# Turning the router's rows in 32x32 blocks on VectorE instead of transposing them on TensorE, in a pool, convolution and mixture-of-experts layer

## The reference, cut to what matters

```python
h = layer_norm(x, ln_in_g, ln_in_b)
mix = hybrid_mixer(h, w_in, pool_w, pool_scale, conv_w, conv_b, w_out)
    # h @ w_in; pooled windows on one half, gated short convolution on the other; @ w_out
h = layer_norm(ALPHA * h + mix, ln1_g, ln1_b)              # called h1 below
probs = softmax(h @ w_router)                              # 16 experts
# the best group of four experts, in it the two best; gates from their probabilities
ffn = grouped_moe(h, ...)          # silu(x @ w1[e]) * (x @ w3[e]) @ w2[e], blocks of 128 rows
h = layer_norm(ALPHA * h + ffn, ln2_g, ln2_b)
```

## Time and the profile before

| what | value |
|---|---|
| median of 3 runs | 1347.22 us (1345.38 to 1347.94) |
| the profiled execution | 1347.38 us, its span in the trace 1345.5 us |
| TensorE busy | 1310.9 us, 97% |
| VectorE busy | 969.2 us, 72% |
| ScalarE busy | 510.8 us, 38% |
| GpSimd busy | 515.4 us, 38% |
| DMA | 243.59 MB, mean 181 GB/s |

### The profile page before, as it was taken

How to read it: one execution, slowest core, us unless ns; L and a number is a source line. 1 busy time by engine, 2 the same in 40 slices (tenths; PEclk the granted TensorE clock), 3 DMA queues, 4 the chain that set the end, 5 groups by cost and what they waited for, 6 DMA issues and landing times.

```text
span 1345.5 us, 20470 instructions
## 1 busy us (share of the span) xinstructions
PE 1310.9 (97%) x6382; PEld 1096.3 (81%) x6383; DVE 969.2 (72%) x1358; ACT 510.8 (38%) x568; POOL 515.4 (38%) x543
## 2 busy tenths in 40 slices
PE   5999999999999999998999999999999999999995
PEld 5888888888888888887888888888888888888884
DVE  7758577687759786698777885775775677777574
ACT  3423234322343234324444554433442454443351
POOL 2001110111101010022566665656555556665655
PEclk9999999999999999999999999999999999999998
DMA  9625434564455344544877774564555545766421
GB/s 271 177 87 164 147 108 169 163 192 117 156 178 167 111 141 146 208 184 167 307 263 266 264 264 145 190 231 140 183 196 186 184 169 210 237 235 233 152 70 64
DMA packets 156523, 243.59 MB, mean 181 GB/s; under 512 B 18944, under 2 KB 84992, under 8 KB 156480
## 3 DMA queue, kind: packets, MB, share of 16 engines
q1 hardware_dynamic: 118624, 154.15, 35.0%
q0 software_dynamic: 28928, 71.74, 15.1%
q10 hardware_dynamic: 8928, 17.13, 3.7%
HBM read 211.97 MB, written 64.62 MB: 206 GB/s over the span
## 4 chain that ended last, share of the span: by engine, by line
PE 94%; DVE 2%; issue 1%; DMA 1%; POOL 1%; DVEq 0%; ACT 0%; SPq 0%; POOLq 0%
PE acc L520 28%; PE acc L522 28%; PE acc L521 28%; PE tp L560 4%; PE logits L599 2%; PE aux L830 1%; DMA b_in<-in_ln_in_b 1%; PE logits L645 0%; DVE ring_lo L1650 0%; DMA xg<-h_scratch,gat_now 0%; DVE ring_lo L1239 0%; PE aux L522 0%; PE aux L521 0%; PE aux L520 0%; PE aux L670 0%
## 5 line engine op out<-in xcount | busy, mean ns | idle before, releaser
L520 PE MATMUL acc<-ring_hi 128*128 128x512 f32 (+1 forms) x800 | 309.1, 386 | 1.8 <-DVE ring_lo L1239 1.6
L522 PE MATMUL acc<-ring_hi,ring_lo 128*128 128x512 f32 (+1 forms) x800 | 305.7, 382 | 0.0
L521 PE MATMUL acc<-ring_lo,ring_hi 128*128 128x512 f32 (+1 forms) x800 | 305.4, 382 | 0.0
L520 PE MATMUL acc<-ring_hi,xt_hi 128*128 128x512 f32 x648 | 256.4, 396 | 2.4 <-issue 2.2
L522 PE MATMUL acc<-ring_hi,xt_lo 128*128 128x512 f32 x648 | 252.8, 390 | 0.0
L521 PE MATMUL acc<-ring_lo,xt_hi 128*128 128x512 f32 x648 | 252.5, 390 | 0.0
L1803 POOL TENSOR_TENSOR small<-small 128x1 f32<-128x1 f32 x31 | 47.4, 1528 | 360.8 <-DVE small L1208 360.8
L520 PEld LDWEIGHTS acc<-ring_hi 128*128 128x128 f32 x800 | 151.4, 189 | 29.9 <-DVE ring_lo L1239 2.4
L522 PEld LDWEIGHTS acc<-ring_hi,ring_lo 128*128 128x128 f32 x800 | 151.3, 189 | 29.1
L521 PEld LDWEIGHTS acc<-ring_lo,ring_hi 128*128 128x128 f32 x800 | 151.5, 189 | 27.6
L1650 DVE TENSOR_TENSOR ring_lo<-stage_x,ring_hi 128x2048 fp32r<-128x2048 f32 x60 | 161.2, 2727 | 0.2
(11 more groups left out here) (277 smaller groups left out, 1922.7 us busy)
## 6 DMA issues: line engine op xcount, KB each, us to landing
stage_x<-in_exp_w SPq DMA_DIRECT2D x64, 1024.0 KB, 6.9
stage<-in_w_in SPq DMA_DIRECT2D x64, 512.0 KB, 5.4
stage<-in_exp_w SPq DMA_DIRECT2D x32, 1024.0 KB, 7.1
stage<-in_w_out SPq DMA_DIRECT2D x32, 512.0 KB, 5.1
h_scratch<-hres POOLq DMA_DIRECT2D x16, 512.0 KB, 3.0
sum_scratch<-hres ACTq DMA_DIRECT2D x16, 512.0 KB, 2.9
hrow<-in_x POOLq DMA_DIRECT2D x12, 512.0 KB, 4.7
h_scratch<-hrow POOLq DMA_DIRECT2D x12, 512.0 KB, 3.0
```

Source lines behind the costliest of these rows:

```text
L520: nc.tensor.matmul(dst, w_hi, x_hi, start=start, stop=False)
L521: nc.tensor.matmul(dst, w_hi, x_lo, start=False, stop=False)
L522: return nc.tensor.matmul(dst, w_lo, x_hi, start=False, stop=stop)
```

## The change

The h1 tiles of the first three routed chunks are no longer transposed by TensorE. ScalarE scales and stores a tile at step `t + 1` already, then loads the unscaled tile back from `h1_dram` into the same place in `hres` at step `t + 2`, in four quarters (`h1_back`): partition quarter `a` gets columns 256a to 256a + 255 of all 128 rows, in pieces of 1 KB. VectorE turns the tile at step `t + 3` with one instruction, in 32x32 blocks, into `h1t` (`h1_turn`, last in the step before the next chunk's layer norm). Column `8 c + k` of the 1024 now lies in block `k`, so `wr` is loaded in that order, and the last chunk's transposes read `hres` with a step of 8. The router matmuls move between the two sections of steps 4 to 7. The residual load of a tile is issued at step `t + 4` and waits for its turn.

```diff
-                if t == 0 and c > 1:
-                    pe.wait_ge(s_h1tc, (c - 1) * TPC * 2)
...
-            def h1_tile(c, t):
-
-                pe.wait_ge(s_h1, c * TPC + t + 1)
-                if t >= 1:
-                    pe.wait_ge(s_h1tc, (c * TPC + t) * 2)
-                transpose_tile(hres[:, t, :], s_h1t)
-
             def route_tile(c, t):
-                pe.wait_ge(s_h1tc, (c * TPC + t + 1) * 2)
+                pe.wait_ge(s_h1turn, c * TPC + t + 1)
...
             def h1_last(t, k):
-                mm = nc.tensor.transpose(last_banks[t % 2][k // 4][:, k % 4, :], hres[:, t, k * P:(k + 1) * P], ident[:])
+                by_k = hres[:, t, :].rearrange("p (c k) -> p k c", k=KT)
+                mm = nc.tensor.transpose(last_banks[t % 2][k // 4][:, k % 4, :], by_k[:, k, :], ident[:])
...
                         section(slot, which, sct).then_inc(s_sec[sct], 1)
+                        if not first and which == 0 and j >= 4:
+                            route_tile(c - 1, j - 4)
...
-                    if not first:
-                        if 3 <= j < 7:
-                            route_tile(c - 1, j - 3)
-                        if 2 <= j < 6:
-                            h1_tile(c - 1, j - 2)
...
-            def h1t_copy(c, t):
-                if c >= 1 and t == 0:
-                    act.wait_ge(s_lst, c)
-                for b in range(2):
-
-                    act.wait_ge(s_h1t, (c * TPC + t) * 2 + b + 1)
-                    nc.scalar.copy(h1t[:, 4 * b:4 * b + 4, :], tp[b][:]).then_inc(s_h1tc, 1)
-
             def alpha_h1(c, t):
 
                 act.wait_ge(s_h1out[t], c * 16 + 16)
-                act.wait_ge(s_h1t, (c * TPC + t + 1) * 2)
+                if c == NCH - 1:
+                    act.wait_ge(s_h1t, (t + 1) * 2)
...
+            def h1_back(c, t):
+
+                act.wait_ge(s_ahout[t], c * 16 + 16)
+                rows = h1_dram[(c * TPC + t) * P:(c * TPC + t + 1) * P, 0:D].rearrange("(r b) (a f) -> a r b f", r=SUB, a=QUARTERS)
+                for a in range(QUARTERS):
+                    dst = hres[a * SUB:(a + 1) * SUB, t, :].rearrange("r (b f) -> r b f", b=QUARTERS)
+                    act.dma_start(dst, rows[a]).then_inc(s_h1q[t], 16)
+
             def res_load(c, t):
 
+                act.wait_ge(s_h1turn, (c - 1) * TPC + t + 1)
...
-                act.dma_start(wr[:], w_router.rearrange("(k p) e -> p k e", p=P)).then_inc(s_const, 16)
+                act.dma_start(wr[:], w_router.rearrange("(p k) e -> p k e", p=P)).then_inc(s_const, 16)
...
-                    if not first and 3 <= j < 7:
-                        h1t_copy(c - 1, j - 3)
+                    if not first and 1 <= j < 5:
+                        alpha_h1(c - 1, j - 1)
+                    if not first and 2 <= j < 6:
+                        h1_back(c - 1, j - 2)
                     if not first and 4 <= j < 8:
-                        alpha_h1(c - 1, j - 4)
-                    if not first and 5 <= j < 9:
-                        res_load(c, j - 5)
+                        res_load(c, j - 4)
...
+
+            def h1_turn(c, t):
+
+                dve.wait_ge(s_h1q[t], (c + 1) * 16 * QUARTERS)
+                dve.wait_ge(s_log, c * TPC + t)
+                if c >= 1 and t == 0:
+                    dve.wait_ge(s_lst, c)
+                V.transpose(h1t[:].rearrange("p k (r b) -> p k b r", r=SUB),
+                            hres[:, t, :].rearrange("p (b c k) -> p k b c", b=QUARTERS, c=SUB)).then_inc(s_h1turn, 1)
...
                     if j < 8 and j % 2 == 1:
                         gate_rows(c, g)
+                    if not first and 3 <= j < 7:
+                        h1_turn(c - 1, j - 3)
```

More of the change, by code:

```diff
@@ L64 @@
 ROW = D + NE
+SUB = 32
+QUARTERS = P // SUB
 ALIGN = 128
@@ L384, in build @@
         s_h1t = sem("h1_transposed")
+        s_h1q = [sem(f"h1_quarters_in{t}") for t in range(TPC)]
+        s_h1turn = sem("h1_quarters_turned")
         s_h1tc = sem("h1_t_copied")
@@ L633, in h1_ready @@
                 elif t >= 2:
-                    pe.wait_ge(s_h1tc, (LAST * TPC + t - 1) * 2)
+                    pe.wait_ge(s_h1tc, (t - 1) * 2)
             def h1_last(t, k):
-                mm = nc.tensor.transpose(last_banks[t % 2][k // 4][:, k % 4, :], hres[:, t, k * P:(k + 1) * P], ident[:])
+                by_k = hres[:, t, :].rearrange("p (c k) -> p k c", k=KT)
+                mm = nc.tensor.transpose(last_banks[t % 2][k // 4][:, k % 4, :], by_k[:, k, :], ident[:])
                 if k % 4 == 3:
@@ L642, in route_last @@
                 if k % 4 == 0:
-                    pe.wait_ge(s_h1tc, (LAST * TPC + t) * 2 + k // 4 + 1)
+                    pe.wait_ge(s_h1tc, t * 2 + k // 4 + 1)
                 tile = LAST * TPC + t
@@ L1077, in _ @@
                 for b in range(2):
-                    act.wait_ge(s_h1t, ((NCH - 1) * TPC + t) * 2 + b + 1)
+                    act.wait_ge(s_h1t, t * 2 + b + 1)
                     if t >= 2:
```

## The result

The changed kernel takes 1415.82 us (median of 4 runs, 1414.07 to 1416.72) beside 1346.54 us for the kernel before: ratio 1.0513, 95% interval 1.0499 to 1.0528, 69.3 us slower. Forecast were 1395 us and at most 1413. The direction and the mechanism came as predicted; the size lies outside the range. The profiled execution has a span of 1414.6 us, 69.1 more than before.

A forecast was written before the change was run, and what follows sets the result against it. TensorE, with 94% of the chain that ended last, was taken as the bound. Stalls 54.0, less 10.9 for removed transposes, plus 3.9 slow clock and 1.0 last chunk, gave +48.0 us: 1395 us, range 1383 to 1413.

The forecast's parts named there:

- the three long waits: TensorE's router tile 0 waits for VectorE's turn once in each of three chunks: 18.6, 17.7 and 17.7 us, together 54.0.
- the ring: ScalarE, VectorE, GpSimd and an h1 store wait on one another once a step; 50.3 us until tile 0 is turned.
- The last chunk's transposes: 32 TensorE transposes kept in the last chunk, reading hres with a step of 8: 1.0 us more, bounds 0 to 3.5.
- each chunk some 14 us longer: A sign named in advance: how much longer each chunk would take if the forecast held.
- first step: ScalarE's issue of a tile's four quarter loads, priced as a plain load's 0.43 us each: 1.7 us a tile.
- The two ScalarE links: ScalarE's scaling, quarter issues and copies before layer norm 2 and before the turn of tile 0: 4.4 and 5.3 us.
- The landings in the ring: Three h1 stores a chunk reach DRAM before ScalarE can go on: 3.0 us each, bounds 2.9 to 4.0.
- the turn: VectorE's new transpose of a 128x1024 f32 tile, counting the strided reading only: 1.9 us, bounds 1.3 to 2.7.
- second step: TensorE running at half clock behind each of three stalls: 1.3 us each, 3.9 us in all, bounds 0 and twice that.
- C: Rival: only VectorE's order counts, ScalarE's waits fit its slack; three stalls of 5.1 us, +7, 1355 us; chance 0.06.
- B: Rival: stores, quarters and scaled stores collide with unit loads; three landings a chunk 2 us longer, 1413 us; chance 0.09.
- D: Rival: tile 0 is turned when TensorE arrives, so the full 10.9 us come back, 1336.5 us; chance 0.03.

The follow-up runs named there:

- experiment 3: Changed kernel with ScalarE's scaling and store, quarter loads and residual load moved behind its bank copies of the same step: 1364.96 us, ratio 1.0146 to the kernel before.
- experiment 11: Kernel before the change, with only the stepped reading of h1 in all 128 TensorE transposes and router weights loaded to match: 1348.57 us, ratio 1.0012.
- experiment 1: Changed kernel with one plain load of a tile in place of four quarters, so tokens go to other experts: 1415.22 us, ratio 1.0507 to the kernel before.
- experiment 2: Changed kernel with GpSimd instead of ScalarE issuing the quarter loads, behind the next tile's h1 store, data unchanged: 1395.98 us, ratio 1.0369 to the kernel before.
- experiment 7: Changed kernel with 90 unused matmuls of 512 columns put ahead of router tile 0 to fill the stall: 1409.45 us, ratio 1.0469 to the kernel before.
- experiment 8: Changed kernel with ScalarE's scale work behind its bank copies, plus 18 unused matmuls before router tile 0 of each chunk: 1359.28 us, ratio 1.0084.
- experiment 6: Changed kernel with ScalarE's scale work behind its bank copies and the router tile at the end of TensorE's step: 1338.12 us, ratio 0.9941.
- experiment 9: Changed kernel with ScalarE's scale work behind its bank copies and VectorE's turn ahead of its layer norm of the step: 1341.89 us, ratio 0.9961.
- experiment 12: Changed kernel with ScalarE's scale work behind bank copies, router tile at the step's end, and GpSimd issuing the quarter loads: 1339.68 us, ratio 0.9945.

## Why the prediction was wrong in size

**Right: what was removed, and the place.** No h1 transpose is left in the first three chunks; the three long waits stand where they were put, one a chunk, and none at tiles 1 to 3. ScalarE's waits for the store are twelve, 8.1 us in the mean and 8.6 at most where 5 to 8 were named, the ring turns as described, and experiment 3 opens it. TensorE ran dry at 210.5 (predicted 209.7). VectorE's links held: from its first pooling instruction to the second store's issue 185.04 to 194.69, 9.65 (9.0 and 0.6), then 203.68 to 210.56, 6.9 (6.3 and 0.6), and 220.34 to 230.63, 10.3 (10.3). The last chunk's transposes cost 0.7 us (from its first xg transposes at 668.45 to the logits' reduce at 685.06, 16.6 us, against 15.9 before), 1.0 predicted; experiment 11 gives 1.6 for four times as many. The sign "each chunk some 14 us longer" was a slip already: the working's own stall and clock, less the transposes, make 15 to 16. Measured from router tile 0 of one chunk to that of the next it is 22 us (205.0 to 353.8 before, 232.8 to 403.4 now).

**Wrong, first step: "the four quarters of tile 0, each as the load issue of 224.08 to 224.51 (0.43), 1.7", and the same for tile 1.** The issue was priced by a plain load's. A plain load kept that price (0.45 in experiment 1), but a quarter took 0.55 to 1.25 us, the four 3.3 and 3.0 us, and this happens twice in the ring before the router waits. The two ScalarE links came out at 6.0 and 6.4 us instead of 4.4 and 5.3. Experiments 1 and 2 measured the term by taking it out: 18.1 us at the mixer's end, 19.8 us in all. That is the whole of the quarters' issue; the forecast had put 3.4 us a chunk, 10 us, of it into the sum. By the rows of the second chunk 3.31 + 3.04 - 3.44 = 2.9 us a chunk were missing, 8.7 in all; by the two experiments 8 to 10. This price had no bounds in the working either, and so the range did not know of it.

**Two smaller parts of the same term.** The landings in the ring were 4.0, 3.0 and 3.3 us where three times 3.0 was taken, and the turn 2.06 to 2.28 us instead of 1.9. The turn lay within its bounds: reading and writing with a step both cost something, 0.97 us together, where I had counted the reading alone, 0.7. With all this the stalls are 22.2, 20.9 and 21.6 us, 64.7 instead of 54.0.

**Wrong, second step: "I charge a stall of 18 us the same, three times: 3.9 us; the bounds are 0 and twice that".** The loss was read off the kernel's start, 1.3 us in a window of 3 us, which says what a half clock costs in three microseconds but not how long it lasts. The window ended inside the slow stretch: in the same trace the matmuls of 256 columns stand 0.21 us apart from 18.04 to 21.67 and 0.12 us from 21.96 on, so read to its end the start loses 1.9 us, and three times that is still less than half of what was lost. Behind the stalls it lasted 8.7 us and cost 4.3 us (4.2 as the mean of the three), 12.5 us in all, above the upper bound of 7.8. Experiments 7 and 8 give most of it back in the trace (8.9 and 7.4 us), though the turn came hardly earlier or later, 6 has no wait above 0.2 us and no slow stretch, and 9 still loses 5.2 us behind two waits of under 1 us. So work in the idle time takes most of the slow clock away; which waits bring it, and how long it then lasts, stays open. The Trainium skill ("TensorE: Matmul & The Clock Gate", part 1) has TensorE fall to half its clock when idle and earn it back by work; the rows agree in direction (0.50 behind the stall, 1.00 later).

**The account.** 65.1 us of waits (64.7 and a last 0.4 at a section) - 10.9 + 12.5 + 0.7 = 67.4 us, of 69.1 between the spans; 1.7 us are not assigned. The forecast's sum was 54.0 - 10.9 + 3.9 + 1.0. So the missing 21 us are 11 in the stalls, of which most is the quarters' issue, 9 in the clock, and the rest unassigned.

**The rivals.** C named a true state: it is what remains when the ring is open (5.4 us a chunk), only that here the ring was closed; its 1355 us had the clock too cheap as well, 2 us for the 11.0 measured, which is 9 of the 10 us by which experiment 3 lies above it. B, transfers that collide, did not happen: the h1 stores land in 2.9 to 4.0 us, median 3.0, as before. Only the scaled stores, on which the ring does not wait, went from a median of 2.9 to 4.3 us. D is reached when both orders are mended, 1338 us where it said 1336.5.

## What to carry to other kernels

When work that waits is moved up in one engine's queue, write down what is queued behind it and who waits for that: ScalarE's wait for a store, placed ahead of two copies, cost 51 of the 69 us here. The cure took a second move with it: the router tile's place, which turned the loss into a gain of 8, or VectorE's turn ahead of its norm, a gain of 5. Price a DMA's issue from a row of its own shape, and give it bounds where there is none. Add to every stall of TensorE what the half clock behind it takes, here 3.2 to 4.6 us, as much for a stall of 5.3 us as for one of 22; behind waits of 0.2 to 2.0 us it was 1.6 to 3.4 us in some places and nothing in others, so give it bounds.

## What the runs showed of the hardware that was not expected

- The issue of a quarter load (32 partitions, four pieces of 1 KB each) held ScalarE 0.55 to 1.46 us, median 0.64 over 48, the second of the four the longest in both tiles of the chain; one plain load of all 128 partitions held it 0.44 us. GpSimd's issue of the same quarter took 0.55 us.
- The slow clock behind a stall of TensorE hardly grew with the stall. At the 1.2 GHz level it ran for 7.9 to 8.7 us behind 20.9 to 22.2 us of idle (the changed kernel), and for 6.5 to 8.6 us behind 5.3 to 5.4 us (experiment 3).
- Behind a short wait and the router tile's sixteen matmuls of 16 columns it came or stayed away, and the length of the wait did not decide it: some 1.8 us were lost behind 1.98 and 2.02 us (experiment 7), 1.43 and 1.36 us (8) and 0.47 us (9), 3.4 us behind 0.95 us (9) and 1.6 us behind 0.26 us (12), but nothing behind 1.29 us (8), 0.65 us (7), 0.24 us (9) and 0.19 us (6).
- VectorE's transpose of 32x32 blocks over 128x1024 f32 took 1.24 us with dense rows, as much as a dense pass, and 2.21 us with a step of 8 elements in reading and 4 in writing.
